# A two-layer hybrid decoder step: three weight blocks at a layer's opening, the decode convolution as products and sums, and a new order

## The reference

```
h = rmsnorm(x, norm_pre);  p = h @ w_in            # 1024 -> 3840, thirty blocks of 128
rq,rk,rv,rg, sq,sk,sv,sg, ca,cb,cg = split(p)
o_r = groupnorm(retention(rope(rq), rope(rk), rv)) * silu(rg)      # 6 heads of 64
o_s = stickbreak(sq, sk, sv, bias) * silu(sg)                      # 6 heads of 64
u   = ca * sigmoid(cb)                                             # 256 channels
o_c = (silu(layernorm(depthwise_conv31(u))) @ pw_w) * silu(cg)
x   = x + rmsnorm(concat(o_r, o_s, o_c) @ w_out, norm_post)
```

## Time and profile before

| | us |
|---|---|
| three runs | 1416.39, 1419.03, 1422.75 |
| median | 1419.03 |
| the profiled execution, its own time | 1421.69 |
| its span, first to last instruction | 1419.2 |

### The profile page before, as it was taken

How to read it: one execution, slowest core, us unless ns; L and a number is a source line. 1 busy time by engine, 2 the same in 40 slices (tenths; PEclk the granted TensorE clock), 3 DMA queues, 4 the chain that set the end, 5 groups by cost and what they waited for, 6 DMA issues and landing times.

```text
span 1419.2 us, 22771 instructions
## 1 busy us (share of the span) xinstructions
PE 1359.9 (96%) x8340; PEld 1168.3 (82%) x8340; DVE 844.4 (60%) x1378; ACT 774.0 (55%) x1535; POOL 526.1 (37%) x446
## 2 busy tenths in 40 slices
PE   6999999999999999999979999999999999999996
PEld 4888888877788887799968888878778888868995
DVE  4338978986523435466762588888865144354665
ACT  6554532746745555665645655336566555556542
POOL 2434351645324433131334435424561244422112
PEclk9999999999999999999999999999999999999998
DMA  6311122210042110455522121131101312006453
GB/s 233 107 48 46 44 66 84 73 52 21 23 123 83 46 30 16 136 184 184 161 83 76 34 61 49 46 131 46 45 16 56 104 47 61 30 16 213 134 175 111
DMA packets 81168, 116.92 MB, mean 82 GB/s; under 512 B 17442, under 2 KB 63010, under 8 KB 80930
## 3 DMA queue, kind: packets, MB, share of 16 engines
q1 hardware_dynamic: 65794, 59.90, 13.4%
q10 hardware_dynamic: 15264, 55.58, 12.1%
HBM read 89.73 MB, written 19.23 MB: 77 GB/s over the span
## 4 chain that ended last, share of the span: by engine, by line
PE 81%; DVE 10%; ACT 3%; issue 3%; POOL 1%; DMA 1%; SPq 0%; ACTq 0%; DVEq 0%; POOLq 0%
PE ring L1113 18%; PE ring L1115 17%; PE ring L1114 17%; PE AV L1263 4%; PE Z L1227 3%; DVE MX L1792 2%; PE Z L1243 2%; PE ring L1136 2%; PE Z L1241 1%; PE ring L1150 1%; PE Z L1257 1%; PE ring L1165 1%; PE ring L1183 1%; PE ring L1154 1%; PE Z L1258 1%
## 5 line engine op out<-in xcount | busy, mean ns | idle before, releaser
L1113 PE MATMUL ring<-H_hi,w_hi 128*128 128x352 f32 x1824 | 613.2, 336 | 15.2 <-DVE H_lo L960 4.9
L1115 PE MATMUL ring<-H_hi,w_lo 128*128 128x352 f32 x1824 | 591.1, 324 | 0.0
L1114 PE MATMUL ring<-H_lo,w_hi 128*128 128x352 f32 x1824 | 590.0, 323 | 0.0
L1113 PEld LDWEIGHTS ring<-H_hi,w_hi 128*128 128x128 f32 x1824 | 346.5, 190 | 54.7 <-issue 35.0
L1114 PEld LDWEIGHTS ring<-H_lo,w_hi 128*128 128x128 f32 x1824 | 347.6, 191 | 4.7 <-issue 1.0
L1115 PEld LDWEIGHTS ring<-H_hi,w_lo 128*128 128x128 f32 x1824 | 346.1, 190 | 0.0
L1983 POOL TENSOR_SCALAR attend<-attend 128x512 f32<-128x512 f32 (+4 forms) x144 | 183.8, 1293 | 199.7 <-ACT attend L1430 199.7
L969 POOL TENSOR_TENSOR w_lo<-w_raw,w_hi 128x1024 fp32r<-128x1024 f32 x58 | 144.8, 2496 | 215.9 <-ACT w_hi L1361 215.9
L1792 DVE SCALAR_TENSOR_TENSOR MX<-MX,vec_sb 128x1005 f32<-128x1005 f32 (+23 forms) x120 | 161.1, 1342 | 1.0
L1665 DVE SCALAR_TENSOR_TENSOR attend<-Z,vec_sb,attend 128x512 f32<-128x512 f32 (+4 forms) x144 | 83.7, 610 | 98.1 <-ACT attend L1438 97.8
L1361 ACT ACTIVATE w_hi<-w_raw 128x1024 fp32r<-128x1024 f32 x82 | 86.7, 1058 | 49.7 <-PE ring L1115 37.0
(11 more groups left out here) (172 smaller groups left out, 1917.5 us busy)
## 6 DMA issues: line engine op xcount, KB each, us to landing
w_raw<-in_w ACTq DMA_DIRECT2D x81, 512.0 KB, 3.5
state<-in_w ACTq DMA_DIRECT2D x25, 512.0 KB, 3.5
out_yT<-MX SPq DMA_DIRECT2D x12, 704.0 KB, 4.4
swapped<-raw_rot SPq DMA_DIRECT2D x144, 44.0 KB, 1.9
attend<-in_cache_k SPq DMA_DIRECT2D x96, 64.0 KB, 2.0
attend<-in_cache_v SPq DMA_DIRECT2D x96, 64.0 KB, 2.1
attend<-in_xT SPq DMA_DIRECT2D x3, 1408.0 KB, 12.5
attend<-out_yT SPq DMA_DIRECT2D x3, 1408.0 KB, 13.2
```

Of the source, the lines that this page charges most:

```text
L1113: nc.tensor.matmul(in_ring(step), a, x, start=(n_k == 0), stop=False)
L1114: nc.tensor.matmul(in_ring(step), a, y, start=False, stop=False)
L1115: last = nc.tensor.matmul(in_ring(step), b, x, start=False, stop=(n_k == KB - 1))
```

## The change

Four things and a new order.

1. The memory of `stop_hi` and `stop_lo` becomes a fourth pair of weight buffers, used for block 2 of each layer. The opening goes (0,c0) (1,c0) (2,c0) (0,c1) (1,c1) (2,c1) (1,c2) (0,c2) (2,c2). The first softplus tile of a layer waits until block 2 has been projected. The first step of each chunk waits for the quarters of that chunk's low part one by one.
2. The 32 decode columns of the convolution leave the taps. A step `taps9` for each block of channels multiplies the 34 rows by the 31 weights for each of the 4 outputs (4 products of 248 columns, laid out in the memory of the prompt's sum before it is used), sums each over the taps (4 reductions from 248 to 8), and adds the bias.
3. The low part of 13 more input blocks of each layer is made on VectorE instead of GpSimd.
4. The last chunk of the last layer is stored in four transfers instead of two.
5. The block order, the costs, dependencies and ranks of the plan are changed, and all five engines' lists with them.

```diff
-BLOCK_ORDER = [("sq", 0), ("sk", 0), ("sv", 0), ("ca", 0), ("cb", 0), ("ca", 1), ("rk", 0), ("cb", 1), ("rv", 0), ("rq", 0),
...
+BLOCK_ORDER = [("sq", 0), ("sk", 0), ("sv", 0), ("ca", 0), ("cb", 0), ("rq", 0), ("ca", 1), ("cb", 1), ("rk", 0), ("rv", 0),
...
+STORES = {(l, c): 4 if (l, c) == (DEPTH - 1, CH - 1) else 2 for l in range(DEPTH) for c in range(CH)}
...
-    return i % LOADS % 2 if i % LOADS < NB else (i % LOADS - NB) % 3
+    n = i % LOADS
+    return 3 if n == 2 else n % 2 if n < NB else (n - NB) % 3
...
+LOW_DVE = [0, 1, 3, 6, 9, 10, 12, 14, 16, 19, 23, 27, 28, 29]
+FIRST_STEPS = ((0, 0), (0, 1), (1, 2))
...
-    return i % LOADS == 1 or i % LOADS >= NB
+    return i % LOADS in LOW_DVE or i % LOADS >= NB
...
-RANKS = {("ACT", "ln_mean"): -1.5, ("ACT", "ro"): 0.5, ("DVE", "log"): 2, ("PE", "ro"): -8, ("DVE", "sample_o"): 1, ("ACT",
...
+RANKS = {("ACT", "ln_mean"): -2.5, ("ACT", "ro"): -0.5, ("DVE", "log"): 2.5, ("PE", "ro"): -2, ("DVE", "sample_o"): 1.5, ("ACT",
...
+                          PEn("proj", c - 1, 0) if c and not l else None, rank=0)
...
-        sequence = [(i, c) for c in range(CH) for i in (0, 1)] + [(i, c) for i in range(2, NB) for c in range(CH)]
+        sequence = [(i, c) for c in range(2) for i in range(3)] + [(1, 2), (0, 2), (2, 2)] + [(i, c) for i in range(3, NB) for c in range(CH)]
...
+            slow = 1.93 if (l, i, c) == (0, 0, 0) else 0.97
+            first = [((helper(q), ("lo", l, c, q)), -slow * q) for q in range(QUARTERS)] if (i, c) in FIRST_STEPS else []
...
+        wide_hi.append(stop_hi[:].rearrange("p a n -> p (a n)"))
+        wide_lo.append(stop_lo[:].rearrange("p a n -> p (a n)"))
...
-                        if n == 0 and n_k % 2 == 0:
+                        if (n, c) in FIRST_STEPS and n_k % 2 == 0:
                             wait_low(pe, "norm", l, c, n_k // 2)
...
+                if i % LOADS == 2 and i > LOADS:
+                    act.wait_ge(s_tot.sem, s_tot.at((i // LOADS * PAIRS - 1, U - 1)))
...
+                    if u == 0 and p % PAIRS == 0:
+                        act.wait_ge(s_full.sem, s_full.at(last_proj(p // PAIRS * LOADS + 2)[1]))
...
+                elif kind == "taps9":
+                    J = step[1]
+                    l, b = divmod(J, CB)
+                    a = V_DW + b * CONV_K
+                    w = vec[:, l, a:a + CONV_K].unsqueeze(1).to_broadcast([P, DEC_BATCH, CONV_K])
+                    n = DEC_BATCH * CONV_K
+                    products = [conv[b][:, n * t:n * t + n].rearrange("p (b k) -> p b k", b=DEC_BATCH) for t in range(DEC_SEQ)]
+                    y9 = conv[b][:, SEQ:NT].rearrange("p (b t) -> p b t", b=DEC_BATCH)
...
+                    for t in range(DEC_SEQ):
+                        nc.vector.tensor_tensor(products[t], glu9[:, b, :, t:t + CONV_K], w, ALU.mult).then_inc(
+                            s_prod9.sem, s_prod9.mark((t, J)))
+                    for t in range(DEC_SEQ):
+                        dve.wait_ge(s_prod9.sem, s_prod9.at((t, J)))
+                        nc.vector.tensor_reduce(y9[:, :, t], products[t], axis=mybir.AxisListType.X, op=ALU.add).then_inc(
+                            s_tap9.sem, s_tap9.mark((t, J)))
...
-                    last = nc.vector.scalar_tensor_tensor(out=y9, in0=glu9[:, b, :, HIST - s:HIST - s + DEC_SEQ], scalar=w,
-                                                          in1=y9, op0=ALU.mult, op1=ALU.add)
-                    last.then_inc(s_tap.sem, s_tap.mark((s, J)))
```

More of the change, by code:

```diff
@@ L386, in plan @@
                 g.add("ACT", ("sqx", l, c, q), 0.85, SPn("x", c, q) if l == 0 else (helper(q), ("res", l - 1, c, q)),
-                      PEn("sum_x", l, c - 1, q // 2) if c else None, rank=2 if c and not l else 0 if c == 2 else 1)
+                      PEn("sum_x", l, c - 1, q // 2) if c else None, rank=3 if c and not l else 0 if c == 2 else 1)
                 if q % 2:
@@ L397, in plan @@
             g.add("ACT", ("part", l, c), 0.45, PEn("sum_x", l, c, 1), PEn("all_x", l, c - 1) if c else None, rank=0)
-            g.add("PE", ("all_x", l, c), 0.65, ACTn("part", l, c), rank=20 if c and not l else 0)
+            g.add("PE", ("all_x", l, c), 0.65, ACTn("part", l, c), rank=0)
             g.add("ACT", ("root_x", l, c), 1.15, PEn("all_x", l, c), rank=0)
@@ L405, in weights @@
                 g.add("ACT", ("wload", W0), 0.45, prev, rank=0, land=3.2)
[L406 to L407 removed]
+                g.add("ACT", ("whi", W0), 1.06, ACTn("wload", W0), last_proj(user_before(W0)) if i != NB + 2 and user_before(W0) is not None else None,
+                      PEn("weigh", l * PAIRS - 1, U - 1) if l and i == 2 else None,
+                      *[POOLn("dec", l * PAIRS + PAIRS - 1, QB), PEn("sample_k", l * PAIRS + PAIRS - 1)] * (i == NB + 2), rank=5 if W0 < 4 else 1 if i < NB else -2)
             else:
@@ L428, in plan @@
                 room.append((before_gate((name, j)), -3.8))
-            last = g.add("PE", step, 3.86, *room, last, first, first2, low_of(base + i) if c == 0 else None, rank=3 if i >= 2 else 0,
-                         lag=-1.5 if i == 0 else 0.0)
+            last = g.add("PE", step, 3.86 if slow < 1 else 7.0, *room, last, *first, low_of(base + i) if c == 0 else None, rank=3 if i >= 3 else 0)
             x = PEn(*step)
@@ L445, in plan @@
                 war = PEn("vtok", *values[n - 1], CH - 1) if n else None
-                g.add("ACT", step, 0.47, x, war, SPn("vout", j) if name == "rv" else None, rank=0)
+                old = [(helper(q), ("res", l - 1, CH - 1, q)) for q in range(QUARTERS)] if l and i == 2 else []
+                g.add("ACT", step, 0.47, x, war, SPn("vout", j) if name == "rv" else None, *old, rank=0)
                 g.drain[step] = ACTn(*step)
@@ L467, in plan @@
             elif name in ("rg", "sg", "cg"):
-                a = g.add("ACT", step, 0.47, x, before_gate((name, j)) if c == 0 else None, rank=0)
+                a = g.add("ACT", step, 0.47, x, before_gate((name, j)), rank=0)
                 src = DVEn("gn_var", j, c) if name == "rg" else DVEn("sample_o", j) if name == "sg" else ACTn("pw", l, c)
@@ L603, in plan @@
                 g.add(e, ("res", l, c, q), 1.0 if e == "DVE" else 1.9, DVEn("post", l, c, q), SPn("oldx", l, c), rank=0 if c == 2 else 2)
-            for h in range(2):
-                g.add("SP", ("store", l, c, h), 0.65, *[(helper(q), ("res", l, c, q)) for q in (2 * h, 2 * h + 1)], rank=1)
+            n = STORES[l, c]
+            for h in range(n):
+                g.add("SP", ("store", l, c, h), 0.65, *[(helper(q), ("res", l, c, q)) for q in range(QUARTERS // n * h, QUARTERS // n * (h + 1))], rank=1)
     squares, prev = [], None
@@ L814, in build @@
         s_tap = sig("s_tap")
+        s_tap9 = sig("s_tap9")
+        s_prod9 = sig("s_prod9")
         s_mid = sig("s_mid")
@@ L1073, in _ @@
                     l, c, h = step[1:]
-                    for q in (2 * h, 2 * h + 1):
+                    n = STORES[l, c]
+                    qs = QUARTERS // n
+                    for q in range(qs * h, qs * h + qs):
                         wait_new(sp, l, c, q)
-                    half = slice(4 * h, 4 * h + 4)
-                    sp.dma_start(io["yT"][:, half, cs(c)], MX[:, half, cs(c)]).then_inc(s_keep.sem, s_keep.mark(l, 16))
+                    rows = slice(2 * qs * h, 2 * qs * h + 2 * qs)
+                    sp.dma_start(io["yT"][:, rows, cs(c)], MX[:, rows, cs(c)]).then_inc(s_keep.sem, s_keep.mark(l, 16))
             sp.wait_ge(s_keep.sem, s_keep.at(DEPTH - 1))
@@ L1498, in _ @@
                                 act.wait_ge(s_vout.sem, s_vout.at(j))
+                        if l > 0 and i % LOADS == 2:
+                            for q in range(QUARTERS):
+                                wait_new(act, l - 1, CH - 1, q)
                         nc.scalar.activation(v_rows[:, cs(c)], src, ACT.Copy).then_inc(s_copy.sem, s_copy.mark(step))
```

74 lines of the change are left out of this document (42 added, 32 removed).

## The result

| | before | after |
|---|---|---|
| median, us | 1417.71 (4 runs, 1415.72 to 1422.75) | 1381.44 (4 runs, 1377.62 to 1383.00) |
| profiled execution, own time and span | 1421.69, 1419.2 | 1383.00, 1381.2 |
| mean granted clock of that execution (lowest to highest of all runs) | 0.981 (0.980 to 0.988) | 0.995 (0.991 to 0.995) |

What follows compares the result with a forecast made beforehand. TensorE, 96% busy, was taken as the bound; 9.7 (layer change) + 2.4 (start) + 3 (decode products, low parts) + 0 (order) + 0.7 (stores) = 15.8 us gave about 1403 us, range 1390 to 1416.

Steps and rivals of the forecast that it cites:

- The bound: Whole kernel: TensorE, busy 1359.9 of 1419.2 us (96%), sets the time; an edit counts by its waits and slow stretches.
- the layer change: Opening of layer 1: the third block fills most of TensorE's idle time and low clock there, gaining 9.7 of 13.1 us.
- the 2.5 named: Sign at the layer change: no TensorE idle time over 2.5 us, and granted clock over 0.9 throughout.
- block 2 is ready in time: Layer change: block 2's load and split are done by 711.4 us, against a need near 716.
- The start: First projection of layer 0: begins at 14.8 us, ends at 21.8 instead of 24.38; gain 2.4 us, bounds 0 and 4.
- decode products and low parts: Stretch of the taps, both layers: a third of TensorE's 5.0 us idle time goes; 3 us, bounds -6 and +8.
- The work on the engines: VectorE near 835 us busy, GpSimd near 460; reductions 0.40 us each; decode convolution 14.4 us in place of 56.7.
- the relief of 42 us: VectorE, decode convolution: dropping 120 instructions over 32 columns for products and reductions relieves it by 42 us.
- The new order: All engines' lists, waits in the middle: counted as zero, from 8 us worse to 8 us better.
- rival 3: Middle of both layers: with lighter GpSimd and shorter taps, half of 23 us idle time goes; 1391 us, chance 12%.
- Rival 4: Taps' stretch: moved low parts crowd VectorE, TensorE waits 1.0 us for each of 26 blocks; 1429 us, chance 10%.
- The last stores: End of kernel: four smaller transfers for the last chunk gain 0.7 us, bounds 0 and 2.

## Why the prediction was wrong

**The bound and the layer change were right.** TensorE was and is the bound. The change of layer was to give 9.7 us; its lost time fell by 10.2, and undoing the block's early steps brings back 8.4 of them. The longest gap left from 712 to 742 is 1.00 us, under the 2.5 named, and the clock is 1.00. That block 2 is ready in time held as well.

**The start was not 2.4 us in this profile.** The first projection was to begin at 14.8; it begins at 17.89, at half clock, and ends near 23. Chunk 0's data came later: ScalarE's squares wait for them 1.95 us, where they waited 1.00 before. First before, then after:
```profile
6.73 1.40 ACT L1390 ACTIVATE gate<-MX 128x352 f32<-128x352 f32 x3 [1.00 <-DMA MX<-in_xT]
```
```profile
7.68 1.41 ACT L1419 ACTIVATE gate<-MX 128x352 f32<-128x352 f32 x3 [1.95 <-DMA MX<-in_xT]
```
In the run with eight more low parts, whose opening is the same, it starts at 14.65 and that stage loses 11.5 us for 15.3; in the one with two stores it starts at 15.46, in the one with sixteen more low parts at 17.75. So the term is real at 3 to 4 us where the load is on time, and 0 where it is late as in this execution.

**The failed step is this sentence: "None of this is on TensorE's path except in the 5.0 us of idle time of that stretch".** For decode products and low parts together I took 3 us. Undoing them in after costs 15.5 and 7.7 us, 23 together; doing both alone in before gives 15.4. The two middles, where these edits act, lost 25.6 us less. That they act in the middle was right, the size was not. The term was mis-sized in two ways:

1. I set it against the 5.0 us of idle time between 100 and 320 and took a third. But VectorE carries softplus in the whole middle, not only beside the taps, and its list is strict, so an instruction taken from ahead of a `stop_lo` can move that tile's sum forward. I had counted 23 us of idle time in the middles and the waits over 0.4 us add up to 23.0; about half, 12.0, went. With the small taps back the waits for `stop_lo` rose from 1.4 to 9.8 us; with the low parts back they didn't rise.
2. I looked for the clock at the start and at the layer change only. Eight more stretches of 3.4 us at 0.5 stood in the middles, some 13.7 us of lost time, and seven of them are gone in after's trace: 12.1 us, as much as the waits themselves. The page's clock row has 9 in nearly every slice and doesn't show them.

The chain on before's page, the work that ended last followed back, had already pointed there: VectorE holds 10% of it, the long taps alone 2%. I read the busy shares and not this line.
```profile
PE 81%; DVE 10%; ACT 3%; issue 3%; POOL 1%; DMA 1%; SPq 0%; ACTq 0%; DVEq 0%; POOLq 0%
```
With the decode products on before's lists VectorE's share is 6%, with the low parts there 5%, and with the small taps back in after 11%. After's own page shows 1%, but its chain is followed over 37% of the span only and can't be set beside these.

**The work on the engines.** The reduction was put at 0.40 us and takes 0.405, like the product of the same length (0.410). Decode products cost 14.0 us in all (6.6 + 6.5, and 1.0 for the additions), forecast 14.4. The low parts moved are 26 of 1.24 us, as forecast. Yet VectorE is 859.8 us busy, not 835, and GpSimd 479.9, not 460: the relief of 42 us was too high. The small taps' 56.7 us lie partly over their neighbours in the trace: without them VectorE's busy time before would be 40.9 us less. And a good part of the 56.7 us is paid beside GpSimd: the 78 small taps that overlap no instruction of GpSimd take 243 ns in the mean, the 42 that overlap one 899. Some operations also got longer without being touched, the clamp on GpSimd from 183.8 to 199.0 us for the same 144. These costs I had at zero, and they were small beside the gain.

**The new order at zero (±8).** Right for the lists alone as far as is known (1419.29 with all edits undone, the decode products left in), wrong as a statement on the sum: 16 us by single terms on old lists became 38 on lists that fit. My rival 3 had the right place ("the middle gains too"), with half of 23 us of idle time as its price and a chance of 12%. Its size was right for the waits, 12.0; the clock in the middle, 12.1, was in none of my terms. That rival 3's 1391 lies nearest to the result is therefore partly luck.

**Rival 4, slower by low parts on VectorE,** was refuted in its strongest form: on before's lists with the small taps still in place, 32 us of subtractions more on VectorE gave 10.5 us less. A block's low part is 1.22 us there and 2.48 on GpSimd. TensorE's wait for low parts stays at 4.8 us, so it is not the shorter subtraction that it was waiting for; the waits for softplus tiles and the half clock fell. **The last stores** bring nothing: two or four, 1379.66 and 1381.44, within the interval, and from the last matmul's start to the end it is 12.2 us with either, although in after a smaller transfer lands sooner, 2.4 us for 3.5 of the ones of 704 KB:
```profile
out_yT<-MX SPq DMA_DIRECT2D x4, 352.0 KB, 2.4
```

## What to carry to other kernels

When the bound engine's clock depends on what it did before, list every stretch at the lower clock over the whole span before pricing an edit: here each cost 1.7 us, the page's clock row didn't show them, and in one pair of executions they were worth as much as the waits. An engine at 60% that holds 10% of the chain that ended last can be on the path: price a relief of it by the bound engine's waits in all stages where it feeds that engine, not in the one where the work is taken out. To find what a part of a replanned kernel is worth, keep its lists and undo the part by hand; planning the half-way kernel anew made it 51 to 135 us slower than the start, which says nothing of what the part is worth. When an undone part leaves work of its replacement behind, its price is an upper bound.

## What the runs showed of the hardware

- 16 matmuls of 4 columns in 1.8 us, with the engine shown as busy, are followed by 3.4 us at half clock at all 6 such places of before, at 5 fewer with 256-column matmuls between them, and at 1 of 6 in after. At 4 of before's 6 places no wait of 0.2 us or more stands in the 5 us ahead.
- A VectorE instruction over 32 columns took 412 to 472 ns in the mean, a reduction from 248 elements 400 to 405, and a product of 248 410 to 471. The mean is made by those beside GpSimd: in before's trace the 78 that overlap no instruction of GpSimd take 243 ns in the mean and 249 at most, the 42 that overlap one 899 and 2385. The long taps behave alike: 1260 ns in the mean and 1276 at most alone (66), 1442 and 3422 beside GpSimd (54). Beside GpSimd the two kinds take 28 and 10 us more, in all, than at the length they have alone.
- The granted-clock column shows 1.00 at after's start, while matmuls of 352 columns start 0.29 us apart until 22.7, as at half clock: at the very start the spacing of the matmuls tells the clock, not the column.
